# Hybrid decoder step: the low parts of fifteen weight chunks written by VectorE instead of GpSimd

## The reference

```python
# per layer, t = 288 tokens in all, D_MODEL = 1024
z = x @ w_in                                   # conv branch, q, six k/v pieces, gates
u = ua * sigmoid(ug)
conv_out = silu(layer_norm(causal_depthwise_conv31(u))) @ w_conv_out
# three attentions over shared q: compressed blocks, selected blocks, window
o = g0 * o_cmp + g1 * o_slc + g2 * o_win
attn_out = o @ w_attn_out
mixed = sigmoid(g_a) * conv_out + sigmoid(g_b) * attn_out
x = layer_norm(ALPHA * x + mixed @ w_o)
x = layer_norm(ALPHA * x + (silu(x @ w_gate) * (x @ w_up)) @ w_down)
```

## Time and profile before

| | |
|---|---|
| median of 3 runs | 1192.49 us |
| the profiled execution | 1188.55 us, span 1186.7 us |
| TensorE busy | 1039.2 us, 88% of the span |
| GpSimd busy | 770.9 us, 65% |
| VectorE busy | 555.3 us, 47% |
| ScalarE busy | 495.1 us, 42% |
| mean granted TensorE clock | 0.936 |

### The profile page before, as it was taken

One profiled execution on the slowest core, in us unless ns is written; L12 is line 12 of the kernel. 1 busy time (PEld: TensorE's weight loads), 2 busy tenths in 40 slices (PEclk: granted clock), 3 DMA queues, 4 the chain that ended last, 5 costly groups with the idle time before them and its releaser, 6 DMA issues.

```text
span 1186.7 us, 22922 instructions
## 1 busy us (share of the span) xinstructions
PE 1039.2 (88%) x7438; PEld 965.6 (81%) x7438; DVE 555.3 (47%) x1070; ACT 495.1 (42%) x902; POOL 770.9 (65%) x1077
## 2 busy tenths in 40 slices
PE   5997798977798999999889968899669799999994
PEld 5996577765787999999779947787558699999993
DVE  2997946435624232210249987543446332222003
ACT  4333345533436544433353232654334364444334
POOL 6998216622493989998559971455127569999882
PEclk9988789988898999999989987999779989999997
DMA  8646458421152664444256534674002324444441
GB/s 305 219 164 216 128 179 281 169 92 54 43 191 82 212 238 163 177 160 169 81 183 219 172 96 133 207 266 174 36 36 102 129 108 160 172 167 160 175 145 76
DMA packets 78140, 185.07 MB, mean 156 GB/s; under 512 B 9283, under 2 KB 42435, under 8 KB 77507
## 3 DMA queue, kind: packets, MB, share of 16 engines
q1 hardware_dynamic: 74130, 171.22, 41.4%
q10 hardware_dynamic: 3744, 11.40, 2.7%
q0 software_dynamic: 144, 0.96, 0.2%
HBM read 170.97 MB, written 12.57 MB: 155 GB/s over the span
## 4 chain that ended last, share of the span: by engine, by line
POOL 63%; issue 35%; POOLq 1%; DMA 1%; ACT 0%; SPq 0%
POOL w_lo L567 57%; POOL hid L590 3%; POOL res L588 2%; POOLq L561 0%; DMA table<-page_table_in 0%; DMA wch<-weights_in 0%; POOLq L585 0%; POOLq L147 0%; POOL hid L588 0%; ACT w_hi L974 0%; POOL hid L591 0%; SPq L429 0%; POOLq L573 0%; SPq L170 0%; POOLq L578 0%
## 5 line engine op out<-in xcount | busy, mean ns | idle before, releaser
L567 POOL TENSOR_TENSOR w_lo<-wch,w_hi 128x256 fp32r<-128x256 f32 x940 | 705.8, 784 | 404.6 <-ACT w_hi L974 402.9
L627 PE MATMUL proj<-x_hi,w_hi 128*128 128x288 f32 x1376 | 416.7, 303 | 39.3 <-DVE x_lo L1598 17.3
L628 PE MATMUL proj<-x_hi,w_lo 128*128 128x288 f32 x1376 | 411.4, 299 | 0.0
L629 PE MATMUL proj<-x_lo,w_hi 128*128 128x288 f32 x1376 | 410.9, 299 | 0.0
L974 ACT ACTIVATE w_hi<-wch 128x1024 fp32r<-128x1024 f32 x235 | 248.3, 1057 | 230.3 <-PE proj L629 118.3
L627 PEld LDWEIGHTS proj<-x_hi,w_hi 128*128 128x128 f32 x1376 | 263.7, 192 | 51.1 <-issue 27.2
L628 PEld LDWEIGHTS proj<-x_hi,w_lo 128*128 128x128 f32 x1376 | 264.5, 192 | 0.0
L629 PEld LDWEIGHTS proj<-x_lo,w_hi 128*128 128x128 f32 x1376 | 263.9, 192 | 0.0
L1295 DVE SCALAR_TENSOR_TENSOR hid<-u_p,sm,hid 128x256 f32<-128x256 f32 x240 | 164.6, 755 | 3.4 <-DVE sq L1324 1.0
L645 PE MATMUL proj<-hid_lo,w_hi 128*128 128x288 f32 x352 | 104.2, 296 | 0.0
L643 PE MATMUL proj<-hid_hi,w_hi 128*128 128x288 f32 x352 | 103.8, 295 | 0.0
(11 more groups left out here) (236 smaller groups left out, 1298.3 us busy)
## 6 DMA issues: line engine op xcount, KB each, us to landing
wch<-weights_in SPq DMA_DIRECT2D x235, 512.0 KB, 3.2
pg<-cmp_pages_in SPq DMA_DIRECT2D x128, 128.0 KB, 2.6
pg<-slc_pages_in SPq DMA_DIRECT2D x128, 128.0 KB, 2.1
wn<-win_in SPq DMA_DIRECT2D x4, 2048.0 KB, 8.4
win_out<-wn ACTq DMA_DIRECT2D x4, 2048.0 KB, 8.1
hid<-w_in SPq DMA_DIRECT2D x2, 1024.0 KB, 5.9
kv_out<-kv ACTq DMA_DIRECT2D x2, 864.0 KB, 5.4
res<-xT_in SPq DMA_DIRECT2D x1, 1152.0 KB, 5.1
```

The source lines that it names most:

```text
L567: last = nc.gpsimd.tensor_tensor(lo[:, cols], raw[:, cols], hi[:, cols].bitcast(F32), ALU.subtract)
L627: mm(ps, hi[:, kb], x_hi[:, kb], start=kb == 0, stop=False)
L628: mm(ps, lo[:, kb], x_hi[:, kb], start=False, stop=False)
L629: last = mm(ps, hi[:, kb], x_lo[:, kb], start=False, stop=kb == KD - 1)
```

## The change

The low parts of chunks 21 to 35 of each layer move from GpSimd to VectorE. VectorE writes each in one instruction of 128 x 1024, at the `fill_out` of output o = n - 2. GpSimd goes from chunk 20 and the convolution straight to chunk 36. A second semaphore, `lo_dve_ready`, counts VectorE's low parts, and `low_of` picks the right one for everyone who waits for a low part: TensorE before a fill, and SyncE before it loads into the slot.

```diff
+LOW_ON_DVE = range(EARLY + 3, CH_IN + 2)
...
-        lo_ready = Signal("lo_ready", CHUNKS)
+        lo_ready = Signal("lo_ready", CHUNKS - len(LOW_ON_DVE))
+        lo_dve_ready = Signal("lo_dve_ready", len(LOW_ON_DVE))
...
+        def low_of(layer, j, back=0):
+
+            if j in LOW_ON_DVE:
+                return lo_dve_ready(layer, j - LOW_ON_DVE.start + 1 - back * lo_dve_ready.per_layer)
+            n = j + 1 if j < LOW_ON_DVE.start else j + 1 - len(LOW_ON_DVE)
+            return lo_ready(layer, n - back * lo_ready.per_layer)
...
-                sp.wait_ge(*lo_ready(layer, user + 1 - back * CHUNKS))
+                sp.wait_ge(*low_of(layer, user, back))
...
-                for n in range(PAIRS, EARLY + PAIRS):
+                for n in range(PAIRS, LOW_ON_DVE.start):
                     low_part(layer, n)
...
-                for n in range(EARLY + PAIRS, CHUNKS):
+                for n in range(LOW_ON_DVE.stop, CHUNKS):
                     low_part(layer, n)
...
-                pe.wait_ge(*lo_ready(layer, j + 1))
+                pe.wait_ge(*low_of(layer, j))
...
                     if o >= O_MIX:
                         merge(o - O_MIX)
+                    elif o + 2 in LOW_ON_DVE:
+                        low_part(o + 2)
+
+                def low_part(n):
+
+                    dve.wait_ge(*hi_ready(layer, n + 1))
+                    hi = w_hi[:, n % PAIRS].rearrange("p k n -> p (k n)")
+                    lo_dve_ready.up(v.tensor_tensor(w_lo[:, n % PAIRS].rearrange("p k n -> p (k n)"),
+                                                    wch[:, n % SLOTS].rearrange("p k n -> p (k n)"), hi.bitcast(F32), ALU.subtract))
```

More of the change, by code:

```diff
@@ L1265, in _ @@
             v = nc.vector
-            owned = (dve_order, conv_lo_ready, attn_lo_ready, hid_lo_ready, nsa_ready, bias_ready, x_lo_ready, x_sum, conv_ready, roped, qs_ready, hs_ready, hin_ready, hg_ready, centered, normed, conv_act,
+            owned = (dve_order, lo_dve_ready, conv_lo_ready, attn_lo_ready, hid_lo_ready, nsa_ready, bias_ready, x_lo_ready, x_sum, conv_ready, roped, qs_ready, hs_ready, hin_ready, hg_ready, centered, normed, conv_act,
                      spread_read, gneg1, gimp, gneg2, gp_ready, gpt_dve, gcopy_ready, go_ready, us_read, uneg, up_ready, uo_ready, mixed_ready)
```

## The result

The changed kernel took 1209.2 us (median of 4 runs, 1207.7 to 1216.1) against 1192.2 us for the kernel before (4 runs). The ratio is 1.0158, with a 95% interval from 1.0132 to 1.0184: slower by 18.8 us, between 15.7 and 21.9.

The account below looks back on a forecast made before the run. Attention from group 0 to unit 3 was taken as bound by TensorE, with GpSimd not the limit. Layer 0 +9.1, layer 1 +8.6, clock +5.7, given back -2.2 sum to +21.2 us: 1192.49 to 1213.7 us, range 1204 to 1221.

Parts of the forecast that it names:

- The place: At group 0, TensorE's fill 22 waits for low part 22, queued on VectorE behind `group_first(0)`, swish, `group_second(0)` and `conv_lo`.
- faster* rival: No stall at fill 22, low part 22 written by 176.0; only GpSimd's silence counts: 1189.4 us, chance 0.04.
- The rule of the Trainium skill: Elementwise work is about twice as fast on VectorE; by that alone the kernel should not get slower.
- Layer 0, +9.1 us and 2.85 for the clock: Fill 22 starts at 187.2, group 0's transposes at 193.9 instead of 184.78: +9.1 us, plus 2.85 for half clock.
- Layer 1, +8.6 us and 2.85: Fill 22 starts at 769.75, group 0's transposes at 776.45 instead of 767.88: +8.6 us, plus 2.85 for half clock.
- The clock, +5.7 us: After the longer pause at fill 22 TensorE works at half clock: +5.7 us for both layers, bounds 3.2 and 8.8.
- loads late* rival: SyncE, held at chunk 25, also loads chunk 26 late for ScalarE: at worst 3.2 us a layer, 1220, chance 0.10.
- less is lost* rival: TensorE's later pauses fall otherwise and units 4 to 7 absorb part of the delay: 1208.0 or 1204, chance 0.12.
- Given back, -2.2 us: VectorE's 128x32 multiply shortens beside silent GpSimd, cutting TensorE's waits in units 1 and 3 by 0.54 each: -2.2 us.
- What costs nothing: Low parts fit VectorE's waits in units, margin 0.25 us; chunk 25's load is harmless; chunk 34 costs 0 to 0.7 a layer.
- The sum: Whole kernel: 9.1 + 8.6 + 5.7 - 2.2 = 21.2 us slower, giving 1213.7 us, 1.8% slower.

Follow-up runs that it names:

- bare wait: Kernel before, all low parts on GpSimd, plus one TensorE wait for VectorE's `conv_lo` ahead of fill 22: 1209.96 us, ratio 1.0152.
- the last experiment: Changed kernel plus 99 transposes of a constant on TensorE ahead of fill 22, into unused columns: 1211.05 us against 1193.04 for the kernel before, ratio 1.0156.
- the doubled work: Only low parts 26 to 33 on VectorE, each written twice in a row: 1188.99 us against 1192.38 for the kernel before, ratio 0.9975.
- the first experiment: Changed kernel with only low parts 26 to 33 on VectorE, the others back on GpSimd: 1189.16 us against 1191.22 for the kernel before, ratio 0.9990.
- 75 transposes: Changed kernel plus 75 transposes of a constant on TensorE ahead of fill 22: 1215.27 us against 1192.38 for the kernel before, ratio 1.0181.
- all others: Changed kernel with low parts 22 to 25 given back to GpSimd; 21 and 26 to 35 stay on VectorE: 1190.46 us, ratio 0.9995.

## Why the prediction was right, point by point

**The place.** Right, and shown from four sides: the stall is there in both layers; it comes with chunks 22 to 25 alone and is gone without them; a bare wait in its place costs as much; and two calls put earlier take it away with all the work left on VectorE. The bare wait is the strongest of the four, since nothing else was changed there. The *faster* rival needed low part 22 ahead of `group_second`. The changed kernel's own list has it behind. With 22 ahead of `group_first(0)` and 23 right behind it, it came to 1.0012, not the gain of 3 us. So moving the work doesn't bring even that gain when all fifteen are moved. The rule of the Trainium skill named in the prediction (GPSIMD Engine Reference, section 8) was again right about the duration, 1.22 us against 2.77 for the four pieces, and says nothing of the sign.

**Layer 0, +9.1 us and 2.85 for the clock.** The multiply took 0.77 us, `conv_lo` 1.36 and a low part 1.22, all as taken. Fill 22 started at 191.57 - 4.38 = 187.2, the time predicted. The two fills took 9.21 us, where 6.7 + 2.85 = 9.55 was taken, and the transposes came 11.6 us late instead of 11.95.

**Layer 1, +8.6 us and 2.85.** Fill 22 started at 786.02 - 16.85 = 769.2 in the time of before, where 769.75 was predicted. VectorE came to `group_second` at 764.5 (781.37 - 16.85) instead of 765.1: the exponentials slipped by 0.25 us and not by 0.85, since the low part of chunk 21 held ScalarE back by 0.75 us and not by 1.22. (ScalarE came to its table load for the group at 770.27 - 16.85 = 753.42 instead of 752.67; VectorE had paused twice there before, for 0.23 and 0.19 us, and the low part filled the pauses.) Together with the fills, which took 8.98 against 9.55 (6.46 of them work, by the last experiment), the transposes came 10.3 us late instead of 11.45. This term was 1.2 us too large.

**The clock, +5.7 us.** Its size at the place is right: 0.50 for 5.60 us in layer 0 and 5.62 in layer 1, half of it lost, 2.8 each (2.5 by the fills at full clock in the last experiment). What isn't shown is that the program as a whole would be 5.6 us shorter without it. With the clock up, the load of chunk 26 came late in both layers, as the *loads late* rival had it, and took 1.1 us of the 2.5 back. Part of the clock's price is then the price of something else that stands ready behind it. In layer 0 1.7 us were left of 2.7, in layer 1 nothing. That the clock falls elsewhere instead, as the *less is lost* rival had it, was seen once, in layer 1, and isn't shown to be a consequence.

**Given back, -2.2 us.** VectorE's 128x32 multiply fell from a median of 717 ns to 184, and the waits ahead of the transposes of units 1 and 3 from 0.68 to 0.16 us. The size is right in the trace: from the transposes of group 0 to the first matmul of group 1 it takes 47.23 us instead of 48.36 in layer 0 and 47.24 instead of 48.31 in layer 1, together 2.2 us. The traces of all kernels with the low parts of the units on VectorE have 9.93 us from unit 0's transposes to unit 1's (10.28 with the doubled work), and those without have 10.46. In the timed medians such an amount can't be told from nothing (-1.2 us [-3.5, +1.2] in the first experiment).

```profile
L1406 DVE TENSOR_TENSOR res<-res,hid x16: 177/184/710, 212.3 to 912.7; 128x32 f32<-128x32 f32 x16
...
819.20 1.09 PE L768 MATMUL ps_t<-cst,res 128*128 128x128 f32 x8 [0.15 <-DVE imp L1407]
```

**What costs nothing.** The units: right, with a wide margin. The load of chunk 25: issued when low part 22 was written, and ScalarE didn't wait for it, not even with the clock up. It didn't wait for that of chunk 26 either, but only because the fills ran at half clock. Chunk 34 was priced at 0 to 0.7 us a layer. Its fill now runs at the end of the pause, at half clock, for 3.05 us instead of 1.7:

```profile
862.27 0.61 PE L669 MATMUL proj<-conv_hi,w_hi 128*128 128x288 f32 x1 [5.99 <-DVE w_lo L1572]
```

From the small sum of group 1 to its transposes it is 9.33 us instead of 8.77, so 0.56 us a layer, within the price; and behind that the clock was full earlier than before, so that unit 4's transposes came 2.2 us (layer 0) and 2.3 us (layer 1) sooner after those of group 1. Another 1.7 and 1.6 us (layers 0 and 1) were lost in group 1 ahead of its small sum, where no wait had changed. There the same page scores ran at half clock; layer 0 before and after:

```profile
233.95 1.94 PE L796 MATMUL ps_s<-pg,qs_rot 128*32 128x512 f32 x16
```

```profile
248.81 3.64 PE L805 MATMUL ps_s<-pg,qs_rot 128*32 128x512 f32 x16
```

This isn't shown to be the price of chunk 34. The trace with 75 transposes has it in both layers too, but three kernels that also write chunk 34 on VectorE (all others, 22 and 23 earlier, the 99 transposes) have nothing of it, and the one with chunks 26 to 33 alone, which doesn't, has 1.6 us in layer 1.

**The sum.** From the profiled execution: 4.4 us up to the small sum of layer 0, 11.6 to the transposes behind it, then 594.22 - 583.10 = 11.1 from there to the transposes of layer 1 (795.00 - 200.78 against 767.88 - 184.78), and 0.5 behind them: 27.6. Without the first 4.4 it is 23.2, and without the two stretches at half clock in group 1 (3.3 us) 19.9, where the sum was 21.2 and the timed medians say 18.8 [15.7, 21.9]. The two don't contradict each other: one execution beside one carries all that varies between executions. The sum lies inside the interval of the measurement. Of its terms, layer 1 is shown to be 1.2 us too large and layer 0 0.3, and what the clock is worth to the whole stays open.

## What to carry to other kernels

An engine works through its list in order, so the cost of giving it one more instruction isn't the instruction's length but the time at which it comes to its turn: look for who waits for the result, and for everything that stands ahead of it in both lists. A 1.2 us subtraction in each layer, put behind two long steps, cost 13 us; put ahead of them, together with the others, it cost nothing that could be measured. A fill that is queued ahead of the step that it was to hide behind must never wait for the engine that makes that step ready, or the two are added instead of overlapped. An average of 47% busy says that an engine has room, never where.

## What the runs showed of the hardware

- The clock of TensorE fell to half in a gap of 3.4 us that followed 17 us of unbroken work at full clock, and it stayed at 0.50 for 5.66 us after work resumed; after the 11.6 us gap of the changed kernel it stayed for 5.62 us, nearly the same. With a gap of 0.80 us it didn't fall. For the time lost when work resumes, the length of these two longer gaps made no difference.
- The clock was also at half in some traces and full in others at the same place of the list. Ahead of group 1's page scores in layer 0 TensorE had worked 1.2 of 2.6 us in the kernel before and in the changed one alike; behind that the clock was 1.00 in the one and 0.50 for 3.3 us in the other, which cost 1.7 us. What decides it isn't shown.
- Beside a silent GpSimd VectorE's instructions were shorter: the 128x32 multiply by a factor of four (717 to 184 ns, medians), the 128x1056 multiply 0.77 instead of 1.20 us, the swish 1.36 instead of 1.78 us. With 36.4 us of low parts added to VectorE, its busy time grew by 18.3.
- The wait for a page load at the start of layer 0's selected attention went from nothing to 4.9 us between traces: none in the kernel before, 1.94, 4.21 and 4.93 us in three kernels whose edits all lie behind it (those that begin with chunk 24 or 26). In the changed kernel the wait of 4.37 us and the half clock behind it cost 7.1 us together. A comparison of two single traces holds such an amount, and it must be read out before the rest is called an effect.
